# A sliding-window attention stage whose rotary partners' rows come by on-chip transfers in place of fp32 products

## The reference, cut to what matters

```
def partial_rope(x, pos):
    half = ROT_DIM // 2
    ...
    x1, x2 = x32[..., :half], x32[..., half:ROT_DIM]
    rot = jnp.concatenate([x1 * cos - x2 * sin, x2 * cos + x1 * sin], axis=-1)
    return jnp.concatenate([rot.astype(x.dtype), x[..., ROT_DIM:]], axis=-1)
...
            q = partial_rope(q, pos)
            k = partial_rope(k, pos)
            y = swa_attention(q, k, v, swa_sinks[j])
            w_out = swa_w_out[j]
        y = y * jax.nn.silu(gate)
        x = x + y @ w_out
    return rmsnorm(x, final_g)
```

## Time and profile before

| | us |
|---|---|
| median of 3 runs | 1783.81 (1783.78 to 1783.83) |
| the profiled execution | 1782.65 |
| its span in the trace | 1780.9 |
| TensorE busy | 1762.0 (99%) |
| VectorE busy | 1311.4 (74%) |
| ScalarE busy | 900.0 (51%) |
| mean granted TensorE clock | 0.998 |

### The profile page before, as it was taken

The page is one execution under the profiler, slowest core; times in us unless marked ns, Lnnn a source line. Parts: engine busy times, 40 slices in busy tenths (PEclk is TensorE's granted clock), DMA queues, the critical chain, the costliest instruction groups (busy, mean ns, idle before and its releaser), DMA issues.

```text
span 1780.9 us, 35710 instructions
## 1 busy us (share of the span) xinstructions
PE 1762.0 (99%) x14365; PEld 1677.1 (94%) x14365; DVE 1311.4 (74%) x2088; ACT 900.0 (51%) x1326; POOL 40.1 (2%) x48
## 2 busy tenths in 40 slices
PE   8999999999999999999999999999999999999997
PEld 8999999999999999999999899998989999999876
DVE  7899899977679987998777765555565656666754
ACT  5433665545533456456565464545455443565553
POOL 0000000000000000000000110100100000000000
PEclk9999999999999999999999999999999999999999
DMA  7666655555666664556566666566655566545553
GB/s 232 189 207 190 190 143 175 191 190 194 196 186 207 192 200 142 155 191 199 180 201 185 203 184 202 181 201 182 195 165 165 191 190 174 155 146 162 161 190 130
DMA packets 199826, 325.54 MB, mean 183 GB/s; under 512 B 14783, under 2 KB 66191, under 8 KB 199565
## 3 DMA queue, kind: packets, MB, share of 16 engines
q1 hardware_dynamic: 197085, 320.85, 58.3%
q10 hardware_dynamic: 2608, 2.84, 0.5%
HBM read 320.42 MB, written 2.69 MB: 181 GB/s over the span
## 4 chain that ended last, share of the span: by engine, by line
PE 94%; DVE 5%; ACT 0%; issue 0%; DMA 0%; DVEq 0%; SPq 0%; ACTq 0%
PE g L495 73%; PE g L506 11%; PE att L641 2%; PE att L620 2%; PE att L596 2%; DVE w_lo L913 2%; DVE cacc L1159 2%; ACT w_hi L1534 0%; PE att L495 0%; PE att L793 0%; DMA stage<-in_w_in_dram 0%; PE att L850 0%; PE att L572 0%; PE att L873 0%; PE att L851 0%
## 5 line engine op out<-in xcount | busy, mean ns | idle before, releaser
L913 DVE TENSOR_TENSOR w_lo<-stage,w_hi 128x1024 fp32r<-128x1024 f32 x577 | 707.3, 1233 | 390.2 <-ACT w_hi L1534 389.3
L1534 ACT CAST w_hi<-stage 128x1024 fp32r<-128x1024 f32 x577 | 599.2, 1050 | 592.6 <-PE g L495 394.4
L495 PE MATMUL g<-a_hi,w_hi 128*128 128x256 f32 x2496 | 704.1, 282 | 2.5 <-DVE w_lo L913 1.6
L495 PE MATMUL g<-a_hi,w_lo 128*128 128x256 f32 x2496 | 693.6, 278 | 0.0
L495 PE MATMUL g<-a_lo,w_hi 128*128 128x256 f32 x2496 | 693.6, 278 | 0.0
L495 PEld LDWEIGHTS g<-a_hi,w_hi 128*128 128x128 f32 x2496 | 470.4, 188 | 12.8 <-issue 10.8
L495 PEld LDWEIGHTS g<-a_hi,w_lo 128*128 128x128 f32 x2496 | 470.3, 188 | 1.5 <-issue 1.2
L495 PEld LDWEIGHTS g<-a_lo,w_hi 128*128 128x128 f32 x2496 | 470.5, 188 | 0.0
L495 PE MATMUL g<-b_hi,w_hi 128*128 128x256 f32 x1440 | 403.1, 280 | 0.4 <-DVE w_lo L913 0.3
L495 PE MATMUL g<-b_hi,w_lo 128*128 128x256 f32 x1440 | 399.9, 278 | 0.0
L495 PE MATMUL g<-b_lo,w_hi 128*128 128x256 f32 x1440 | 399.9, 278 | 0.0
(11 more groups left out here) (231 smaller groups left out, 1378.3 us busy)
## 6 DMA issues: line engine op xcount, KB each, us to landing
stage<-in_fox_w_in_dram SPq DMA_DIRECT2D x128, 512.0 KB, 4.1
stage<-in_w_in_dram SPq DMA_DIRECT2D x112, 512.0 KB, 3.9
stage<-in_swa_w_in_dram SPq DMA_DIRECT2D x72, 512.0 KB, 3.8
stage<-in_w_in_dram SPq DMA_DIRECT2D x128, 256.0 KB, 3.1
stage<-in_w_out_dram SPq DMA_DIRECT2D x64, 512.0 KB, 4.3
stage<-in_w_pg_dram SPq DMA_DIRECT2D x64, 512.0 KB, 4.1
stage<-in_fox_w_out_dram SPq DMA_DIRECT2D x32, 512.0 KB, 4.6
stage<-in_swa_w_out_dram SPq DMA_DIRECT2D x32, 512.0 KB, 4.3
```

Source lines behind the costliest of these rows:

```text
L495: mm = pe.matmul(acc[:, j * S:(j + 1) * S], w[:, slot, c0 + j * P:c0 + (j + 1) * P], xx[:, k, :], start=st and m == 0 and j % 2 == 0, stop ...
L913: dve.tensor_tensor(w_lo[:, slot, :], stage[:, slot, :], w_hi[:, slot, :].bitcast(F32), ALU.subtract).then_inc(*t.inc("w_split"))
L1534: act.copy(w_hi[:, slot, :], stage[:, slot, :]).then_inc(*t.inc("w_rounded"))
```

## The change

The products of `turn_q` go, with their waits. In their place ScalarE issues four transfers a turn from `q` to `turned`, each 8 partitions by 1024 elements (32 KB): rows 0 to 7 from rows 8 to 15 and the other way, for both heads of the pair. They stand at ScalarE's hook 1 (behind the cast of piece 4), after a wait for the scaled `q`. VectorE's step at hook 2 now waits for all four (`q_swapped`, 64). It reads 1024 elements a partition from `turned` in SBUF where it read 2 x 512 from PSUM. For the keys the product stays. Behind the keys' step VectorE once negates sin in rows 0 to 7 of each head and clears `turned`. ScalarE's gate step waits for one `gemm_free` where it waited for two, because the new step takes the other; the awaited event is the same.

```
-            def turn_q():
-                taken()
-                pe.wait_ge(*t.again("s_free"))
-                pe.wait_ge(*t.again("t_free"))
-                pe.wait_ge(*t.again(misc_reader[0]))
-                misc_reader[0] = "rope_used"
-                pe.matmul(MB[:, :], rot, q[:, 0:2, :].rearrange("p a b -> p (a b)"), start=True, stop=True)
-                pe.matmul(SB[:, :], rot, q[:, 2:4, :].rearrange("p a b -> p (a b)"), start=True, stop=True).then_inc(*t.inc("roped"))
...
-                chunk("T", A, 0, work={4: [turn_q]} | swa_scores())
+                chunk("T", A, 0, work=swa_scores())
...
+                dve.wait_ge(*t.own())
+                for base in (0, HD):
+                    dve.tensor_scalar(rope[base:base + 8, 1, :], rope[base:base + 8, 1, :], -1.0, None, ALU.mult).then_inc(*t.inc("dve_step"))
+                dve.memset(turned[:, :, :], 0.0).then_inc(*t.inc("turned_zero"))
+
+            def q_rotary():
+                dve.wait_ge(*t.see("q_swapped", 64))
+                dve.tensor_tensor(turned[:, :, :], turned[:, :, :], spread(rope[:, 1, :], 0, CT), ALU.mult).then_inc(*t.inc("dve_step"))
+                dve.tensor_tensor(q[:, :, :], q[:, :, :], spread(rope[:, 0, :], 0, CT), ALU.mult).then_inc(*t.inc("dve_step"))
+                dve.wait_ge(*t.own())
+                dve.tensor_tensor(q[:, :, :], q[:, :, :], turned[:, :, :], ALU.add).then_inc(*t.inc("q_roped"))
...
+            def swap_q():
+
+                act.wait_ge(*t.see("gemm_free"))
+                act.wait_ge(*t.again("turned_zero"))
+                for base in (0, HD):
+                    for a, b in ((0, 8), (8, 0)):
+                        fetch(turned[base + a:base + a + 8, :, :], q[base + b:base + b + 8, :, :], "q_swapped")
...
             with t.loop(act, "swa", 3) as g:
-                chunk()
+                chunk({1: [swap_q]})
...
-                       7: [gate_silu(2)]})
+                       7: [gate_silu(1)]})
```

More of the change, by code:

```diff
@@ L61 @@
     "swa": dict(
-        act_step=9, att_done=8, dve_step=19, gate_act=1, gemm_done=16, gemm_free=2, keys_in=48,
+        act_step=9, att_done=8, dve_step=20, gate_act=1, gemm_done=16, gemm_free=2, keys_in=48,
         maxed=1, mb_free=1, normed=8, o_ready=2, ob_free=1, operand_ready=1, ot_done=2, ot_used=1,
-        pt_done=8, q_roped=1, rope_used=1, roped=1, s_free=9, scored=8, t_free=8, w_rounded=16,
+        pt_done=8, q_roped=1, q_swapped=64, s_free=8, scored=8, t_free=8, w_rounded=16,
         w_split=16, w_used=16, weights_ready=8, y_rounded=1),
@@ L235, in two_blocks @@
             sq_done ssq_done stat_done var_ready rs_ready rs_spread rs_taken ln_spread p_in p_turned p_split h_new e_ready
-            keys_ready keys_swapped keys_out keys_in sig_ready
+            keys_ready keys_swapped q_swapped turned_zero keys_out keys_in sig_ready
             f_done f_used lf_step lf_turned lf_by_token lf_ln cum_done cum_used ck_ready ck_out roped rope_used q_ready
@@ L842, in turn_keys @@
                 t.skip("rope_used")
-            def turn_q():
-                taken()
-                pe.wait_ge(*t.again("s_free"))
-                pe.wait_ge(*t.again("t_free"))
-                pe.wait_ge(*t.again(misc_reader[0]))
-                misc_reader[0] = "rope_used"
-                pe.matmul(MB[:, :], rot, q[:, 0:2, :].rearrange("p a b -> p (a b)"), start=True, stop=True)
-                pe.matmul(SB[:, :], rot, q[:, 2:4, :].rearrange("p a b -> p (a b)"), start=True, stop=True).then_inc(*t.inc("roped"))
-                t.skip("rope_used")
-                t.skip("s_free")
             def swa_there():
@@ L1424, in _, with keys_rotary @@
                             step()
[L1427 to L1438, removed]
+            def keys_rotary():
+                x_ = kk[:, 0, :].rearrange("p (j s) -> p j s", j=2)
+                dve.wait_ge(*t.see("roped"))
+                dve.wait_ge(*t.own())
+                dve.tensor_tensor(turned[:, 0:2, :], MB[:, :].rearrange("p (j s) -> p j s", j=2),
+                                     spread(rope[:, 1, :], 0, 2), ALU.mult).then_inc(*t.inc("rope_used"))
+                dve.tensor_tensor(x_, x_, spread(rope[:, 0, :], 0, 2), ALU.mult).then_inc(*t.inc("dve_step"))
+                dve.wait_ge(*t.own())
+                dve.tensor_tensor(x_, x_, turned[:, 0:2, :], ALU.add).then_inc(*t.inc("keys_roped"))
+                dve.wait_ge(*t.own())
+                for base in (0, HD):
+                    dve.tensor_scalar(rope[base:base + 8, 1, :], rope[base:base + 8, 1, :], -1.0, None, ALU.mult).then_inc(*t.inc("dve_step"))
+                dve.memset(turned[:, :, :], 0.0).then_inc(*t.inc("turned_zero"))
@@ L1440, in swa_scores @@
             def swa_scores():
-                hooks = {0: [evac(1, scaled(q[:, :, :], QSCALE))], 2: [turn_rotary(q[:, :, :], 4, (MB, SB), "q_roped")]}
+                hooks = {0: [evac(1, scaled(q[:, :, :], QSCALE))], 2: [q_rotary]}
                 for j in range(GH):
@@ L1450, in _ @@
             chunk({2: [var()], 3: [take_rs, evac(0, keys_values())],
-                   6: [turn_rotary(kk[:, 0, :].rearrange("p (j s) -> p j s", j=2), 2, (MB,), "keys_roped")]})
+                   6: [keys_rotary]})
             with t.loop(dve, "swa", 3) as g:
@@ L1806, in _ @@
             chunk({2 * g + 1: [copy_rows(g)] for g in range(4)})
+            def swap_q():
[4 more added lines that the diff above has]
+                        fetch(turned[base + a:base + a + 8, :, :], q[base + b:base + b + 8, :, :], "q_swapped")
             chunk({7: [keys_out]})
+            t.skip("turned_zero")
             with t.loop(act, "swa", 3) as g:
-                chunk()
+                chunk({1: [swap_q]})
                 chunk({0: [exps("swa", (0, 1, 2, 3))], 1: [exps("swa", (4, 5, 6, 7))], 3: [copy_turned("swa", (0, 1))],
                        4: [copy_turned("swa", (2, 3))], 5: [copy_turned("swa", (4, 5))], 6: [copy_turned("swa", (6, 7))],
-                       7: [gate_silu(2)]})
+                       7: [gate_silu(1)]})
                 high_of(gate[:, :, :], B[0][:, bass.ds(g * CT, CT), :], "mb_free")()
-            chunk()
+            chunk({1: [swap_q]})
             chunk({0: [exps("swa", (0, 1, 2, 3))], 1: [exps("swa", (4, 5, 6, 7))],
                    3: [copy_turned("swa", (0, 1))], 4: [copy_turned("swa", (2, 3))],
-                   5: [copy_turned("swa", (4, 5)), gate_silu(2)],
+                   5: [copy_turned("swa", (4, 5)), gate_silu(1)],
                    6: [copy_turned("swa", (6, 7))], 7: [high_of(gate[:, :, :], B[0][:, 12:16, :], "mb_free")]})
```

## The result

| | before | after |
|---|---|---|
| median of 6 runs, us | 1783.8 (1782.51 to 1784.57) | 1797.79 (1795.0 to 1798.9) |
| profiled execution / its span, us | 1782.65 / 1780.9 | 1797.39 / 1795.6 |
| mean granted TensorE clock | 0.998 | 0.994 |

The ratio of after to before is 1.0078, with a 95% interval of 1.0065 to 1.0091. 7.7 us of work have left TensorE and the kernel is 14 us slower. The forecast was 1783.3 us, with a range up to 1788.5.

The account below looks back on a forecast made before the run. TensorE was taken as the bound, busy 99% of the span; 7.7 us leave it and 7.2 come back as waits, -0.5 us together, so 1783.3 us against a median of 1783.81, range 1781.0 to 1788.5.

Parts of the forecast that it names:

- The removed work: On TensorE, two fp32 products a turn leave the chain in the last stage, 7.66 us over four turns.
- The place of the wait: TensorE ahead of the first scores: waits of about 2.4 us in turns 1 to 3, none or small in turn 0.
- The issue: On ScalarE, between the casts of pieces 4 and 5: 0.50 us for each of four transfers, 2.0 us together.
- The landing: Fourth transfer, from issue until its rows are in `turned`: 2.8 us taken, rows bounding it by 1.6 and 4.4.
- a rival with a chance of 12%: At VectorE's wait ahead of the rotary step: fourth transfer lands late behind weight loads, slower by 3.6 us or more; 12%.
- x: Time from the scaled `q` to `q_roped` in each turn, forecast at 8.1 us.
- The text's own formula: Change at the scores: turns 1 and 2 x - 7.78 each, turn 3 x - 7.49, turn 0 -1.72 up to 8.59.
- The turning point for "slower": Over the four turns, slower by 3.6 us needs x = 9.24, a landing 4.0 us after issue.
- The clock: Rival on TensorE: each wait doubles the time of the following 16 score products, 4.5 us in all, 1787.8 us; chance 4%.
- A late landing of 4.4 us: Dear end of the forecast: 0.58 us an issue and 4.4 to landing, x = 9.91, +6.3 us, 1790.1 us.
- The robust value: Scaled `q` to `q_roped`, by piece 5's split 7.97 us, by the fourth transfer 8.07; 8.1 used as robust.
- Its signs of being wrong: In the profile: issue under 0.3 or over 0.7 us, landing over 4 us, no VectorE wait, or the clock falling.

Follow-up runs that it names:

- slots 11 and 14: The changed kernel with the two score batches in slots 11 and 14 instead of 8 and 12; 1775.3 us against 1783.25 before, ratio 0.9957, in its second measurement.
- the products as mere work: The changed kernel with two fp32 products a turn put back in slot 4, their results read by nobody; 1796.85 us against 1787.63 before, ratio 1.0065.

## Why the prediction was wrong, point by point

- **The removed work** was sized right: 7.66 us forecast, 7.7 us found in the stage with slots 11 and 14.
- **The place of the wait** was right: TensorE waits ahead of the scores for the sum into `q`, VectorE waits for `turned<-q`. That nothing is disturbed elsewhere (the later cast and split, the later loads, the clearing of `turned`) held too. The clearing took 0.91 us and the two sign changes 0.28 each.
- **The issue** was the first term mis-sized: 0.50 us taken, bounds 0.34 to 0.58, measured 0.64 (median of 16), outside the bounds, and 1.25 for the first one of turn 0. Four of them are 2.6 us.
- **The landing** was the second: 2.8 us taken, measured 4.50, 3.70, 3.42 and 3.35. "A little less since each carries a quarter" is the step that failed. The 512 KB weight loads beside the transfers weren't in the term, only in a rival with a chance of 12%; with loads of 64 KB the same four land in 2.3 us, so the loads are 1.1 to 2.2 us of it in turns 0 to 2.
- **So x**, the time from the scaled `q` to `q_roped`, was 10.8 (the 10.9 in an expectation above is rounded from the start of the scores), 9.4, 9.1 and 9.0 us and not 8.1. The text's own formula with these values gives +0.5, +1.6, +1.3 and +1.5, +5.0 us, and 5.9 was measured. Of the difference 0.6 us is the step from the end of the sum to the first score, 0.12 us in turns 0 to 2 and 0.24 in turn 3, which the formula leaves out. The arithmetic carried, the inputs didn't. The turning point for "slower" was written down as x = 9.24. Turn 0 was to gain 1.7 us and lost 0.9: its landing took 4.50 us, against 2.30 with small weight loads.
- **The clock** was the third, and the dearest: 4% chance, 4.5 us. It cost 6.2 us. The reason against it, that idling of over 3 us was needed and the waits were 2.4, held for the 2.59 us of turn 0, but it was read from one stretch and is no bound: another kernel lost its clock after 2.16 us. The failed step is to hold the late landing and the clock as separate rivals with chances that add. The second follows from the first: each tenth of a microsecond that the landing was late brought the wait nearer to the length at which the clock goes. A late landing of 4.4 us was priced at +6.3; with the clock it is some 12, outside the range.
- **The robust value** wasn't: that both paths gave x within 0.1 us of each other rested on one shared guess, the issue, and said nothing of its error. It passes through four times.
- **Its signs of being wrong** did show it: the clock fell in three turns, and in turn 0 the landing took over 4 us and the first issue over 0.7.

In one sentence: the mechanism was named, its size was taken from the cheap side of the rows twice, and the price behind the wait was taken as linear where it has a step.

## What to carry to other kernels

When work leaves the bounding engine and a chain of transfers takes its place, ask first when the result is due and move its consumer by as much as the chain is longer: here two numbers in a slot list turned a loss of 14 us into a gain of 8. Price several small transfers by the sum of their bytes and issues beside the bulk stream that runs at that time, not by the size of one. And price a wait on TensorE together with the clock: here every wait of 3.5 us and more lost it, shorter waits mostly kept it, but one of 2.16 us did not, and where the clock was lost a wait cost up to twice what it lasted.

## What the runs showed of the hardware

- **The clock against the idle stretch.** Over the kernels above, in the last stage, where TensorE idled ahead of scores, it kept the clock over stretches of up to 2.59 us in all cases but one, of 2.16 us, and over one of 3.08; it lost it with one of 3.03 and with every one of 3.50 us and more. So the length of the one stretch does not settle it, and what does stays open here. What it cost in the changed kernel was 1.4 us on 16 score products and 0 to 1.0 us behind them.
- **Four transfers of 8 rows beside weight loads.** From the start of the fourth issue they land in 2.3 us beside loads of 64 KB and in 3.4 to 4.5 us beside loads of 512 KB.
- **An issue of ScalarE** with 8 or 16 rows of 4 KB from on-chip to on-chip takes 0.61 us (16 rows, median) or 0.64 (8 rows), longer than one of 64 rows of 2 KB (0.58). In turn 0 the first one takes 1.25 us in every kernel with 8 rows; with 16 rows it takes 0.62 there. I have no explanation for that.
- **Two spacings of weight products.** 132 of them take 15.18 us or 15.75 us a turn, at full clock and without a wait, and it changes from kernel to kernel and from turn to turn (in the kernel before 15.18 in turn 1; in the kernel with the products as mere work 15.75 in turns 0 to 2). Up to 0.6 us a turn hangs on it, which is the size of what was left unexplained above. Its cause stays open.
